# Identity products taken out of both mixing stages of a two-layer encoder trunk

## What is computed

```python
h = layer_norm(x, ln_in_w, ln_in_b)
for l in range(2):
    proj = h @ w_in[l]
    y = concatenate([retention(p_ret), s5(p_s5), hyena(p_hy), mlstm(p_ml)])
    h = layer_norm(DN_ALPHA * h + y @ w_out[l], ln1_w[l], ln1_b[l])
    f = swiglu(h, ...) if l == 0 else moe_swiglu(h, ...)
    h = layer_norm(DN_ALPHA * h + f, ln2_w[l], ln2_b[l])
```

```python
s = einsum(q, k) * exp(dmat - m_row)       # decay weights from running maxima of the gates
num = einsum(s, v);  den = sum(s)
h = num / maximum(abs(den), exp(-m_row))
```

## Time and profile before

| what | value |
|---|---|
| median of 3 runs | 1670.68 us (1670.31 to 1671.7) |
| profiled execution, its own time | 1669.8 us |
| its span, first to last instruction | 1667.9 us |
| TensorE busy | 1618.3 us, 97% |
| VectorE, ScalarE, GpSimd busy | 1355.2, 943.1 and 55.5 us |
| mean granted clock of TensorE | 0.993 of full speed |
| stages by time from the start | first mixing 18 to 232, dense 244 to 457, second mixing 460 to 649, experts from 668 |

### The profile page before, as it was taken

How to read it: one execution, slowest core, us unless ns; L and a number is a source line. 1 busy time by engine, 2 the same in 40 slices (tenths; PEclk the granted TensorE clock), 3 DMA queues, 4 the chain that set the end, 5 groups by cost and what they waited for, 6 DMA issues and landing times.

```text
span 1667.9 us, 18694 instructions
## 1 busy us (share of the span) xinstructions
PE 1618.3 (97%) x7666; PEld 1269.4 (76%) x7666; DVE 1355.2 (81%) x1447; ACT 943.1 (57%) x959; POOL 55.5 (3%) x39
## 2 busy tenths in 40 slices
PE   7998999999999999999999999999999999999996
PEld 5645758988756676788888888888888888888885
DVE  6899467765657956788888898988998989988898
ACT  4321316644312132677777777777777777777773
POOL 0111000000011100000000000000000000000000
PEclk9999999999999999999999999999999999999998
DMA  7230253643433125699988999989999989999981
GB/s 321 101 148 4 88 208 149 244 183 147 182 133 151 51 92 237 232 371 373 365 350 343 366 363 374 360 339 358 361 358 374 362 346 352 385 368 373 361 334 47
DMA packets 40604, 444.24 MB, mean 266 GB/s; under 512 B 4416, under 2 KB 4544, under 8 KB 7360
## 3 DMA queue, kind: packets, MB, share of 16 engines
q1 hardware_dynamic: 39360, 438.78, 67.4%
q10 hardware_dynamic: 1152, 4.19, 0.6%
HBM read 437.71 MB, written 5.24 MB: 266 GB/s over the span
## 4 chain that ended last, share of the span: by engine, by line
PE 85%; DVE 10%; ACT 3%; issue 1%; DMA 0%; SPq 0%; DVEq 0%
PE bank L1123 34%; PE bank L1150 16%; PE bank L1002 8%; PE bank L603 5%; PE bank L616 4%; PE bank L1011 3%; PE bank L812 3%; DVE ring_lo L2038 2%; PE bank L1131 1%; DVE ring_lo L2168 1%; PE bank L774 1%; ACT ex_up_hi L1414 1%; PE bank L1071 1%; PE bank L1094 1%; PE bank L761 1%
## 5 line engine op out<-in xcount | busy, mean ns | idle before, releaser
L2038 DVE TENSOR_TENSOR ring_lo<-ring,ex_up_hi 128x2048 fp32r<-128x2048 f32 x224 | 512.8, 2289 | 51.1 <-ACT ex_up_hi L1414 49.6
L1414 ACT ACTIVATE ex_up_hi<-ring 128x2048 fp32r<-128x2048 f32 x224 | 429.2, 1916 | 113.1 <-PE bank L1123 105.9
L1123 PE MATMUL bank<-ex_up_hi,ex_x_hi 128*128 128x512 f32 x896 | 361.9, 404 | 6.3 <-DVE ring_lo L2038 4.7
L1123 PE MATMUL bank<-ring_lo,ex_x_hi 128*128 128x512 f32 x896 | 350.6, 391 | 0.0
L1123 PE MATMUL bank<-ex_up_hi,ex_x_lo 128*128 128x512 f32 x896 | 350.1, 391 | 0.0
L2168 DVE TENSOR_TENSOR ring_lo<-ring,ex_w_hi 128x2048 fp32r<-128x2048 f32 x111 | 253.1, 2280 | 0.0
L1522 ACT ACTIVATE ex_w_hi<-ring 128x2048 fp32r<-128x2048 f32 x111 | 211.6, 1907 | 0.0
L1123 PEld LDWEIGHTS bank<-ex_up_hi,ex_x_hi 128*128 128x128 f32 x896 | 168.4, 188 | 44.5 <-DVE ring_lo L2038 13.8
L1123 PEld LDWEIGHTS bank<-ring_lo,ex_x_hi 128*128 128x128 f32 x896 | 168.2, 188 | 36.1
L1123 PEld LDWEIGHTS bank<-ex_up_hi,ex_x_lo 128*128 128x128 f32 x896 | 168.8, 188 | 30.5
L1150 PE MATMUL bank<-ex_w_hi,ex_mid_hi 128*128 128x512 f32 x448 | 174.5, 389 | 0.0
(11 more groups left out here) (330 smaller groups left out, 2110.0 us busy)
## 6 DMA issues: line engine op xcount, KB each, us to landing
ring<-moe SPq DMA_DIRECT2D x112, 2048.0 KB, 7.6
ring<-moe SPq DMA_DIRECT2D x112, 1024.0 KB, 7.4
ring<-ffn SPq DMA_DIRECT2D x11, 3072.0 KB, 10.0
win<-w_in SPq DMA_DIRECT2D x12, 2048.0 KB, 8.4
win<-w_out SPq DMA_DIRECT2D x4, 2048.0 KB, 10.2
lnb<-ln SPq DMA_DIRECT2D x4, 1024.0 KB, 6.0
tab<-yT ACTq DMA_DIRECT2D x8, 512.0 KB, 5.6
pr<-par SPq DMA_DIRECT2D x2, 1728.0 KB, 12.1
```

What stands on the lines that cost most here:

```text
L1123: ins = mm(b[:, :], ex_x[x % 3][x_][:, k, :], (ex_up_hi, lo)[w_][:, k, :], start=(k == 0 and m == 0), stop=(k == KT - 1 and m == 2))
L1414: act(ex_up_hi[:, HS * q:HS * (q + 1), :], wt[:, HS * q:HS * (q + 1), :], ACT.Copy).then_inc(e_uh, 1)
L2038: tt(ring_lo[s][:, half], ring[s][:, half], hi.bitcast(F32), ALU.subtract).then_inc(e_ul, 1)
```

## The change

Thirteen calls of `keep_busy` are deleted from TensorE's lists, seven in `mix_0` (26 products: 2, 4, 4, 4, 4, 4 and 4) and six in `mix_1` (24 products). Every other call stays where it was, and so do the `keep_busy` calls outside the two mixing stages. No other engine's list changes.

```diff
@@ mix_0 of TensorE
                 ret_out(0, 3)
-                keep_busy(2, 6)
                 unit(0, 5)
...
                 ml_scores(0, 1)
-                keep_busy(4, 6)
-                keep_busy(4, 6)
                 ml_out(0, 0)
-                keep_busy(4, 4)
                 ml_scores(0, 2)
-                keep_busy(4, 4)
-                keep_busy(4, 4)
                 ml_out(0, 1)
-                keep_busy(4, 4)
                 ml_scores(0, 3)
```

## The result

The changed kernel takes 1679.05 us in the median of 6 runs (1676.34 to 1684.01), the kernel before 1670.73 us (1670.31 to 1671.7) in as many. The ratio is 1.0048, 95% interval 1.0036 to 1.0061: **slower by 0.5%**, where 0.6% faster was forecast.

A forecast was written before the change was run, and what follows sets the result against it. TensorE was taken to bound both mixing stages; gains of 5.5 and 3.7 us, waits taken off and the clock at 0, sum to 9.2: 1670.68 - 9.2 = 1661.5 us. Own range 1659 to 1664, reaching up to 1671.5 with rival 1's cases.

The forecast's parts named there:

- What bounds the kernel: Both mixing stages: TensorE sets the pace, busy 48.07 of 49.00 us and 50.68 of 51.70 us at full clock.
- Cost of the products: Both mixing stages: the deleted identity products take 0.245 us each, 12.2 us in all, the upper bound of the direct gain.
- New waits: Among the heads: waits take back 0.85 us in the first stage; the second's first two groups gain only 0.18 of 1.88.
- Behind the stages: From the mLSTM norm on: the 2.15 us of slack stay and everything moves together, costed at nothing.
- rival 3: At the mLSTM norm: its chain keeps its place, so each stage gains only 2.15 us of slack; 1666.4 us, chance 0.05.
- The clock: TensorE in both stages without identity products: keeps its full level of 2.4 GHz, so the loss is taken as 0.
- Rival 1: Among the heads: clock falls some 10 us per stage, then returns with the output products; 1669.4 us, chance 0.33.
- Rival 2: Both stages: half level lasts 15 us in each, 3.6 us slower, 1674.3 us; slower beyond 22.7 us together; chance 0.12.

The follow-up runs named there:

- e5: Kernel before with four identity products wherever eight stood and without the two ahead of the projection unit: 1670.95 us against 1670.85, ratio 0.9995.
- e3: Kernel before with the products of all thirteen calls kept in place but run on 4 rows of the array: 1699.9 us, ratio 1.0166.
- e4: Kernel before with the products of all thirteen calls kept on 128 rows but with 32 columns of weights: 1672.77 us, ratio 1.0013.

## Why the prediction was wrong

- **What bounds the kernel**: right. TensorE sets both stages, and its rate shows at once in the time.
- **Cost of the products** (12.2 us in all): nearly right. In the changed kernel the first output starts at the end of the second head's scores, where 1.89 us stood between. In e5, whose level stayed full in the first stage, eight products fewer shorten the stretch from the first scores to its end from 48.96 to 230.97 - 183.79 = 47.18 us, 0.22 us each instead of 0.245.
- **New waits**: right for the first two groups of the second stage (0.7 us before L655 and 0.9 before L729; measured 0.53 and 0.76, with 0.22 before L812 between them). The waits of 0.4 us in the first stage and of 0.45 us before the fourth head in the second never came, since the level fell first; no run shows them.
- **Behind the stages**: right. The idle time at the mLSTM norm's transposes stayed zero, and the 0.93 us behind it stayed as well, in both stages; rival 3 thus had no case.
- **The clock: this step failed.** It said: "I take 0, because the row nearest in busy share, 13 to 18 us, held the clock with far more idle time." Busy share was the wrong measure. That stretch holds transposes and identity products on 128 rows; the heads hold products on 64 and 4 rows and of 65 columns. The term stood at 0 in the sum; the stages ran 17.07 and 23.90 us at half level, and half of that, some 20 us, is what it should have held before the waits that vanish in it. e3 shows that 4-row products in the same places, with no wait added in the first stage, do not hold the level, e4 that products on 128 rows do in most executions. The text named this very difference and then chose the row by the other one.
- **Rival 1** had the place and the mechanism, and put 10 us of half level into each stage; 17.1 and 23.9 us were measured. What it missed is that the level does not come back among the heads, where output products stand alone between thin work; it came back only with the output products around the last outputs. That thin work, spread over twice the time at half level, cannot bring it back is the likely reason, and was not tried by itself.
- **Rival 2** is what happened. Its rule, half of the time at half level less 2.15 us of waits and 9.2 us of gain, gives (17.07 + 23.90) / 2 - 11.35 = 9.1 us for the profiled execution of the changed kernel; measured are 10.6 us between the profiled executions (8.3 between the medians). The rule lets all waits vanish, and the 1.5 us of the second stage, which stand ahead of the fall, did not. Its point of decision, 22.7 us, was passed by far. Its chance, 0.12, was too low: it hung on the row chosen above.
- The rule of the Trainium skill (TensorE: Matmul & The Clock Gate, "HAM oscillation") that was weighed there, which lays falls to long idle gaps, does not account for this fall: in the first stage the level fell at 193.58 with TensorE busy 2.98 of 2.98 us before it and 17.07 of 17.07 us during it.

## What to carry to other kernels

Before filler products are taken out, look at what stands beside them, by rows of the array and by columns streamed, not by busy share: a stretch that shows 100% busy can be thin. Put useful full-row products between thin ones first, and look at what is then left to fill; here output products between the heads and a fuller router gave back a third of a percent and narrower runs, and the share of the fill in it is not shown. A filler in front of a real wait was nearly free here (0.14 us), and taking two such groups out cost 1.5 us. Look at the granted clock of every run, not of one profile: the level falls in some executions of a kernel and not in others.

## Not expected of the hardware

- Identity products on 4 rows of the array did not hold the full level: 24 of them were streamed among the heads of each stage, and the half level lasted 27.3 and 34.1 us. Those on 128 rows and 32 columns held it in both stages of the profiled execution; two of ten runs, at a mean clock of 0.987, suggest that they do not always.
- At half level the float32 score products take 1.9 times as long (2.00 for 1.05 us), the outputs of 65 columns 2.1 times (2.76 for 1.29 us). The earlier trace rows has 1.74 times for products of 256 columns on 128 rows and 32 columns; the first 0.35 of the 3.33 us of that row ran at full level.
- Whether the level falls differs from execution to execution of the same kernel, and by it the time: 1665.98 to 1682.64 us with half of the fill, 1666.39 to 1668.17 us with output products and fill between the heads and eight products at the router.
